# Squares of the differential heads summed in two rounded parts, and the next values' parts moved ahead, in a two-layer transformer kernel

## The chip, the cores and the metric

The kernel runs on one core of one Trainium2 chip. The metric is the device time of one execution in microseconds (us). The engines are TensorE (PE, matrix products; its weight loads are listed apart as PEld), VectorE (DVE), ScalarE (ACT), GpSimd (POOL) and SyncE (SP, which issues the DMAs). Each engine runs its own instruction list in order and waits on semaphores for the others.

## The reference, cut to what matters

Two transformer blocks are computed for 512 tokens of width 1024. The second block is where the change lies. It projects its normed input to two attentions, one with block selection (here a plain masked softmax of eight heads) and one with four differential heads:

```python
def diff_attention(q, k, v, lam, slopes):
    ...
        p = jax.nn.softmax(sc, axis=-1)
        a = p[:, :, 0] - lam * p[:, :, 1]
        return jnp.einsum('bhqk,bhkd->bhqd', a.astype(v.dtype), v)
...
d_out = rms_norm(d_out, diff_subln[layer]) * (1.0 - lambda_init)
...
mixed = jnp.concatenate([m_out, d_out], axis=-1)[:, :S]
x = x + jnp.einsum('bse,ed->bsd', mixed, w_out[layer])
```

The `rms_norm` of each differential head needs, for each token, the sum of the squares of the head's 128 outputs. That sum is what is changed.

## The kernel before, in words

All data lie transposed: 128 channels on the partitions, 512 tokens in a row. Large products are made in three terms: each operand is split into a rounded part of type fp32r (`_hi`) and the remainder (`_lo`), and TensorE adds high x high, low x high and high x low (lines 463 to 465, `products`). Plain f32 matmuls are used for transposes by the identity and for a few sums.

The second attention goes over eight chunks of 128 channels, c = 0 to 7. Even chunks are differential heads (`is_diff`), odd ones are pairs of ordinary heads. The loop `for c in range(0, KC, 2)` stands in the program of each engine, each with an order written out by hand, and all order between engines is by semaphores. What belongs to the pair c, c+1 around the change:

- `values2(c)` (PE) multiplies the transposed probabilities by the values into `OUT_BANK`; `raw_out(c)` (DVE, line 2267) copies that to `att2[:, 0]`; `square_out(c)` (ACT, line 1535) squares it into `d_sq`; `square_sum(c)` (PE) sums the squares over the partitions with a matrix of ones (line 1012, one f32 matmul of 512 columns) and adds an epsilon term that carries the softmax denominators, `rx_d`, by four f32 matmuls of 128 columns (line 1014); `variance(c)` (DVE) scales the sum to `d_v`; `first_root(c)` (ACT, lines 1540 and 1542) and `root(c)` (DVE, its first instruction writes `d_sq` from `d_y`) make the norm, and `gated_out(c)` (POOL, line 2547) applies the gate.
- The values of chunk c+2: `value_transposes(c + 2)` (PE, line 911) turns them, `stage_v2(c + 2)` (ACT, line 1495) makes `vd_hi`, `value_low(c + 2)` (DVE) makes `vd_lo` and raises `v2_lo_ready`. `value_half(c + 3, 0)` (PE, twelve matmuls of 512 columns) overwrites the bank that they read and so waits for `v2_lo_ready`.
- The probabilities of chunk c+1, first head: `transposes(c + 1, 0)` (PE, line 951, ten transposes) writes them to `PT_BANK`, `high_probs(c + 1, 0)` (ACT, line 1520) and `low_probs(c + 1, 0)` (DVE) split them. `transposes(c + 1, 1)` writes the second head's to the same bank, and waits for `low_probs(c + 1, 0)` by `ptl_ready`.

After the last pass PE forms the output projection by `out_chunks(t, first, last)`: t is the tile of the output and first, last are the mixed chunks it covers. `low_out(t)` (POOL, line 2563) makes the low part of its weights. `hold` on POOL is an instruction of one element (line 2518) that stands ahead of the remainders it makes (line 2521).

Of the kernel before, what the change touches and what calls it, by code (L numbers as in the profile page):

```python
# [8 lines left out]
F32R = mybir.dt.float32r  # L9
# [5 lines left out]
P = 128  # L15
# [65 lines left out]
def two_layer_block(nc, xT, vecs, wstream, outT):  # L81
    with ExitStack() as ctx:
# [12 lines left out]
        def sem(name):  # L95
            return ctx.enter_context(nc.semaphore(name))
# [120 lines left out]
        s2 = put("s2", [P, 2, 1280], F32)  # L217
        v_t = put("v_t", [P, T], F32)
        d_v = put("d_v", [P, T], F32)
        rx_d = put("rx_d", [P, TB, P], F32)  # L220
        rx_m = put("rx_m", [P, TB, P], F32)
        pt_hi = put("pt_hi", [P, 1280], F32R)
# [24 lines left out]
        def out_weights(t):  # L247
# [47 lines left out]
        out_read, raw_copied, dsq_ready, dss_ready, dvar_ready, drs_ready, d_final, att2_final, mixed_ready = (  # L295
            sem("out_read"), sem("raw_copied"), sem("dsq_ready"), sem("dss_ready"), sem("dvar_ready"),
            sem("drs_ready"), sem("d_final"), sem("att2_final"), sem("mixed_ready"))
        pool_held, gap_zeroed = sem("pool_held"), sem("gap_zeroed")
        first_done, first_sq, first_acc, first_drained = (
            sem("first_done"), sem("first_sq"), sem("first_acc"), sem("first_drained"))  # L300
# [159 lines left out]
        def _(pe):  # L460
# [420 lines left out]
            def value_half(c, half):  # L881

                if c >= KC:
                    return
                n = v_unit(c)
                if half == 0:
                    if c < 2:
                        pe.wait_ge(tile_drained, CREDIT + T_Q2 + 15 + c)
                    elif c == 2:
                        pe.wait_ge(g_drained, 1)  # L890
                    else:
                        pe.wait_ge(v2_lo_ready, c)
                    pe.wait_ge(lo_ready, n + 1)
                for k in range(4 * half, 4 * half + 4):
                    w = slice(k * P, (k + 1) * P)
                    mm = products(ps[:, v_bank(c), :], w_hi[:, n % 2, w], w_lo[:, n % 2, w], a_hi[:, k, :], a_lo[:, k, :],
                                  first=k == 0, last=k == KC - 1)
                if half:
                    mm.then_inc(units_done, 1)
# [106 lines left out]
            def square_sum(c):  # L1006

                if c >= KC:
                    return
                pe.wait_ge(dsq_ready, c // 2 + 1)  # L1010
                pe.wait_ge(rx_ready, c + 1)
                pe.matmul(ps[:, OUT_BANK, :], ones[:, :], d_sq[:, :], start=True, stop=False, skip_group_check=True)
                for b in range(TB):
                    mm = pe.matmul(ps[:, OUT_BANK, b * P:(b + 1) * P], rx_d[:, b, :], ident[:, :], start=False,
                                   stop=b == TB - 1, skip_group_check=True)
                mm.then_inc(dss_ready, 1)

            def out_chunks(t, first, last):

                high, low = out_weights(t)  # L1020
                if first == 0:
                    pe.wait_ge(lo_ready, U_W2 + t + 1)
                for n in range(first, last):
                    pe.wait_ge(mixed_ready, n + 1)
                    j = W2_ORDER[n]
                    w = slice(j * P, (j + 1) * P)
                    mm = products(ps[:, W2_BANKS[t], :], high[:, w], low[:, w], b_hi[:, j, :], b_lo[:, j, :],
                                  first=n == 0, last=n == KC - 1)
                if last == KC:
                    mm.then_inc(units_done, 1)  # L1030
# [34 lines left out]
            for c in range(0, KC, 2):  # L1065
                transposes(c)
                if c:
                    value_transposes(c + 1)
                scores2(c + 1, 0)
                if 0 < c < KC - 2:  # L1070
                    value_half(c + 2, 0)
                    value_half(c + 2, 1)
                    scores2(c + 1, 1)
                    gate_half(c + 1, 0)
                    scores2(c + 1, 2)
                    gate_half(c + 1, 1)
                else:
                    gate_half(c + 1, 0)
                    scores2(c + 1, 1)
                    gate_half(c + 1, 1)  # L1080
                    scores2(c + 1, 2)
                values2(c)
                value_transposes(c + 2)
                transposes(c + 1, 0)
                if c + 2 < KC:
                    square_sum(c)
                    value_half(c + 3, 0)
                    scores2(c + 2, 0)
                    transposes(c + 1, 1)
                    scores2(c + 2, 1)  # L1090
                    value_half(c + 3, 1)
                    scores2(c + 2, 2)
                    values2(c + 1, 0)
                    gate_part(c + 2, 0, 5)
                    values2(c + 1, 1)
                    den_rows(c + 1)
                    gate_part(c + 2, 5, KC)

            square_sum(KC - 2)
            pe.wait_ge(g_drained, KC)  # L1100
            out_chunks(0, 0, KC - 2)
            transposes(KC - 1, 1)
            values2(KC - 1, 0)
            pe.wait_ge(s2_biased, 4 * 16)
# [15 lines left out]
        def _(act):  # L1120
# [411 lines left out]
            def square_out(c):  # L1532

                act.wait_ge(raw_copied, c // 2 + 1)
                act.activation(d_sq[:, :], att2[:, 0, :], ACT.Square).then_inc(dsq_ready, 1)

            def first_root(c):
# [54 lines left out]
            for c in range(0, KC - 2, 2):  # L1592
                if c:
                    high_probs(c - 1, 1)
                    exponentials(c, 2)
                    high_mixed(c - 2)
                    split_unit(v_unit(c + 2))
                    split_unit(g_unit(c + 1))
                    stage_v2(c + 1)
                high_probs(c)  # L1600
                if c:
                    high_mixed(c - 1)
                exponentials(c + 1, 0)
                if c:
                    split_unit(v_unit(c + 3))
                exponentials(c + 1, 1)
                stage_qk2(c + 2)
                exponentials(c + 1, 2)
                square_out(c)
                stage_v2(c + 2)  # L1610
                high_probs(c + 1, 0)
                gate_sigmoid(c + 1)
                split_unit(g_unit(c + 2))
                gate_sigmoid(c)
                exponentials(c + 2, 0)
                first_root(c)
                exponentials(c + 2, 1)
                stage_qk2(c + 3)
# [29 lines left out]
        def _(dve):  # L1648
# [584 lines left out]
            def low_probs(c, head=0):  # L2233
                if c >= KC:
                    return
                dve.wait_ge(pth_ready, tq_of(c, head) + 1)
                low(pt_lo[:, :], psf[:, PT_BANK * 512:PT_BANK * 512 + 1280], pt_hi[:, :]).then_inc(ptl_ready, 1)
# [22 lines left out]
            def raw_out(c):  # L2260

                if c >= KC:
                    return
                dve.wait_ge(av2_ready, tq_of(c) + 1)
                if c:
                    dve.wait_ge(mixed_ready, c - 1)
                dve.tensor_copy(att2[:, 0, :], ps[:, OUT_BANK, :]).then_inc(raw_copied, 1)

            def variance(c):

                dve.wait_ge(dss_ready, c // 2 + 1)
                ts(d_v[:, :], ps[:, OUT_BANK, :], 1.0 / P, ALU.mult).then_inc(dvar_ready, 1)
# [44 lines left out]
            for c in range(0, KC, 2):  # L2317
                biased(c + 1, 0)
                low_probs(c)
                if c:  # L2320
                    value_drain(c + 2)
                den_small(c)
                den_spread(c)
                biased(c + 1, 1)
                if 0 < c < KC - 2:
                    biased(c + 1, 2)
                    gate2_drain(c + 1)
                else:
                    gate2_drain(c + 1)
                    biased(c + 1, 2)  # L2330
                raw_out(c)
                den_small(c + 1)
                den_spread(c + 1)
                slopes(c + 2)
                value_low(c + 2)
                variance(c)
                low_probs(c + 1, 0)
                biased(c + 2, 0)
                biased(c + 2, 1)
                value_drain(c + 3)  # L2340
                root(c)
                biased(c + 2, 2)
                low_probs(c + 1, 1)
                joined(c + 2, (3, 2, 0, 1))
                gate_row(c + 1)
                gate2_drain(c + 2)
                slopes(c + 3)
                value_low(c + 3)
                if c + 2 < KC:
                    gated(c + 1)  # L2350
# [355 lines left out]
```

## Time and profile before

| | |
|---|---|
| median of 3 runs | 1016.03 us (1015.81 to 1016.11) |
| profiled execution, its own time | 1016.16 us |
| its span | 1014.0 us |
| PE busy | 1002.1 us, 99% |
| DVE / ACT / POOL busy | 557.6 / 454.1 / 502.3 us |
| mean granted TensorE clock | 1.0 of full speed |

The span is the time from the first to the last instruction that the profiler recorded; the execution's own time is 2.2 us longer. Starts in the timeline are in us from the start of the span. Matmuls overlap in the pipeline: the time that one costs PE is the distance to the start of the next, not its own listed duration. In a bracket stands the time that the engine sat idle before an instruction and who ended it.

### The profile page before, as it was taken

How to read it: one execution, taken by the hardware profiler on the slowest of the kernel's cores; microseconds unless marked ns; L12 is line 12 of the kernel's file. 1: busy time of each engine (PE TensorE's matmuls, PEld its weight loads, DVE VectorE, ACT ScalarE, POOL GpSimd, SP SyncE). 2: the span in 40 equal slices, each digit the busy share in tenths (PEclk: the TensorE clock that was granted, in tenths of full speed). 3: DMA queues.
4: the chain of work that ended last, by engine and by line, in shares of the span. 5: the costliest groups of instructions: out<-in, count | busy, mean ns of one | idle time of the engine just before them, and what ended most of it. 6: DMA issues, size and time to landing. Idle time of an engine off the chain costs nothing.

```text
span 1014.0 us, 13704 instructions
## 1 busy us (share of the span) xinstructions
PE 1002.1 (99%) x5051; PEld 835.4 (82%) x5051; DVE 557.6 (55%) x943; ACT 454.1 (45%) x682; POOL 502.3 (50%) x296
## 2 busy tenths in 40 slices
PE   9999999999999999999999999999999999999998
PEld 7888888888888988888888888889888778777787
DVE  6799897887633964334334310116715276676731
ACT  7222346898644532322322322233454347667630
POOL 4444365842346134444444465453387545755562
PEclk9999999999999999999999999999999999999999
DMA  7232222212244032332322323333132120111112
GB/s 258 83 104 93 95 83 67 80 63 84 73 176 151 17 102 86 103 101 85 103 100 87 103 104 104 104 123 106 43 104 83 63 84 22 64 63 43 42 63 83
DMA packets 26402, 91.11 MB, mean 90 GB/s; under 512 B 3056, under 2 KB 3184, under 8 KB 26224
## 3 DMA queue, kind: packets, MB, share of 16 engines
q1 hardware_dynamic: 26352, 90.42, 26.4%
q8 instruction: 34, 0.56, 0.2%
q14 instruction: 16, 0.13, 0.0%
HBM read 88.31 MB, written 2.10 MB: 89 GB/s over the span
## 4 chain that ended last, share of the span: by engine, by line
PE 89%; DVE 7%; ACT 2%; issue 1%; DMA 1%; POOL 0%; SPq 0%; DVEq 0%
PE ps L463 27%; PE ps L465 27%; PE ps L464 27%; PE ps L927 2%; PE ps L951 1%; DVE resid L2014 1%; PE ps L624 1%; PE ps L640 1%; DVE a_lo L1664 1%; DMA resid<-x_t 1%; DVE sq_x L1657 1%; DVE q_raw L1657 1%; DVE mix L1657 1%; DVE b_lo L1664 1%; PE ps L656 0%
## 5 line engine op out<-in xcount | busy, mean ns | idle before, releaser
L2362 POOL TENSOR_TENSOR w_lo<-w_raw,w_hi 128x1024 fp32r<-128x1024 f32 x137 | 325.8, 2379 | 410.6 <-ACT w_hi L1128 357.9
L1128 ACT ACTIVATE w_hi<-w_raw 128x1024 fp32r<-128x1024 f32 x133 | 139.2, 1047 | 279.6 <-PE ps L465 279.6
L463 PE MATMUL ps<-a_hi,w_hi 128*128 128x512 f32 (+1 forms) x544 | 211.6, 389 | 4.6 <-DVE v_lo L1661 3.1
L465 PE MATMUL ps<-a_hi,w_lo 128*128 128x512 f32 (+1 forms) x544 | 207.0, 380 | 0.0
L464 PE MATMUL ps<-a_lo,w_hi 128*128 128x512 f32 (+1 forms) x544 | 206.8, 380 | 0.0
L463 PE MATMUL ps<-b_hi,w_hi 128*128 128x512 f32 x392 | 152.9, 390 | 0.0
L465 PE MATMUL ps<-b_hi,w_lo 128*128 128x512 f32 x392 | 152.6, 389 | 0.0
L464 PE MATMUL ps<-b_lo,w_hi 128*128 128x512 f32 x392 | 152.5, 389 | 0.0
L463 PEld LDWEIGHTS ps<-a_hi,w_hi 128*128 128x128 f32 x544 | 102.3, 188 | 28.3 <-DVE v_lo L1661 4.4
L465 PEld LDWEIGHTS ps<-a_hi,w_lo 128*128 128x128 f32 x544 | 102.3, 188 | 20.0
L464 PEld LDWEIGHTS ps<-a_lo,w_hi 128*128 128x128 f32 x544 | 102.4, 188 | 18.3 <-issue 0.2
L463 PEld LDWEIGHTS ps<-b_hi,w_hi 128*128 128x128 f32 x392 | 73.6, 188 | 15.2
L464 PEld LDWEIGHTS ps<-b_lo,w_hi 128*128 128x128 f32 x392 | 73.6, 188 | 15.2
L465 PEld LDWEIGHTS ps<-b_hi,w_lo 128*128 128x128 f32 x392 | 73.6, 188 | 15.2
L1741 DVE SCALAR_TENSOR_TENSOR ps<-u_pad,vec,ps 128x512 f32<-128x512 f32 x112 | 75.4, 747 | 0.0
L463 PE MATMUL ps<-h_hi,w_hi 128*128 128x512 f32 (+1 forms) x186 | 69.2, 372 | 0.0
L464 PE MATMUL ps<-h_lo,w_hi 128*128 128x512 f32 (+1 forms) x186 | 69.0, 371 | 0.0
L465 PE MATMUL ps<-h_hi,w_lo 128*128 128x512 f32 (+1 forms) x186 | 69.0, 371 | 0.0
L1657 DVE TENSOR_TENSOR up_h<-up_u,up_s 128x512 f32<-128x512 f32 x22 | 51.3, 2330 | 21.2 <-ACT up_s L1387 21.1
L1657 DVE TENSOR_TENSOR up_u<-ps,scale_row 128x512 f32<-128x512 f32 x22 | 15.2, 690 | 82.0 <-PE ps L465 82.0
L1657 DVE TENSOR_TENSOR sq_f<-sq_f 128x512 f32<-128x512 f32 x13 | 12.5, 960 | 82.7 <-ACT sq_f L1411 82.0
L1508 ACT ACTIVATE s<-s,smax 128x384 f32<-128x384 f32 (+2 forms) x64 | 35.2, 552 | 16.9 <-DVE smax L2187 16.9
(339 smaller groups left out, 1727.1 us busy)
## 6 DMA issues: line engine op xcount, KB each, us to landing
w_raw<-weights SPq DMA_DIRECT2D x156, 512.0 KB, 3.2
resid<-x_t SPq DMA_DIRECT2D x8, 256.0 KB, 6.6
w_raw<-weights SPq DMA_DIRECT2D x8, 256.0 KB, 6.6
resid<-x_t SPq DMA_DIRECT2D x1, 2048.0 KB, 8.8
out_t<-out_sb SPq DMA_DIRECT2D x8, 256.0 KB, 2.0
vec<-vecs SPq DMA_DIRECT2D x1, 220.0 KB, 7.1
vec<-vecs SPq DMA_DIRECT2D x1, 4.0 KB, 1.6
```

The lines of the kernel that those rows point to most:

```text
L463: pe.matmul(out, s_hi, m_hi, start=first, stop=False, skip_group_check=True)
L464: pe.matmul(out, s_hi, m_lo, start=False, stop=False, skip_group_check=True)
L465: return pe.matmul(out, s_lo, m_hi, start=False, stop=last, skip_group_check=True)
L624: pe.matmul(z_of(h)[:, o:o + (b + 1) * P], q[r, tok], k[r, keys], start=b != 0 and t == 0, stop=False, skip_group_check=True)
L640: mm = pe.transpose(z_of(h)[:, o:o + P], neg_log[:, src:src + P], ident[:, :])
L927: mm = pe.matmul(scores_of(part, head, b), q2[rows, tok], k2[rows, keys], start=n == 0 and t == 0, stop=False, skip_group_check=True)
L1128: act.activation(w_hi[:, k % 2, 0:width], w_raw[:, k, 0:width], ACT.Copy).then_inc(hi_ready, 1)
L1508: e = act.activation(s2[:, head, w], s2[:, head, w], ACT.Exp, scale=-1.0, bias=smax[:, head, b:b + 1], accum_out=den[:, kind_of(c), half_o ...
L1657: return dve.tensor_tensor(out, in0, in1, op)
L1664: return dve.scalar_tensor_tensor(out=out, in0=in0, scalar=scale, in1=high.bitcast(F32), op0=ALU.mult, op1=ALU.subtract)
L1741: V.do(dve.scalar_tensor_tensor(out=acc if k == TAPS - 1 else part, in0=src, scalar=w, in1=part, op0=ALU.mult, op1=ALU.add))
L2362: pool.tensor_tensor(w_lo[:, k % 2, 0:width], w_raw[:, k, 0:width], w_hi[:, k % 2, 0:width].bitcast(F32), ALU.subtract).then_inc(lo_ready, 1)
```

## The change

The square sum is made from two parts. ACT writes the square twice, rounded to fp32r (`d_hi`) and in f32 (`d_sq`); DVE subtracts them to `d_lo` (`square_low`); PE sums both parts with two fp32r matmuls of 512 columns in place of one f32 matmul. The two new tiles lie in the places of `d_v` and `d_y`, which are not in use then.

The orders change. PE: `value_half(c + 3, 0)` stands ahead of `square_sum(c)` in the passes c = 0, 2, 4; after the last pass, `out_chunks(0, 0, KC - 2)` stands ahead of `square_sum(KC - 2)`. ACT: `stage_v2(c + 2)` stands ahead of `square_out(c)`. DVE: `value_low(c + 2)` stands right behind `raw_out(c)`, ahead of the denominators, then `square_low(c)`; in the last pass alone, `variance` stands behind `low_probs`.

```diff
+        d_hi = place("d_hi", [P, T], F32R, at["d_v"])
+        d_lo = place("d_lo", [P, T], F32R, at["d_y"])
...
-                pe.wait_ge(dsq_ready, c // 2 + 1)
+                pe.wait_ge(dsq_lo, c // 2 + 1)
                 pe.wait_ge(rx_ready, c + 1)
-                pe.matmul(ps[:, OUT_BANK, :], ones[:, :], d_sq[:, :], start=True, stop=False, skip_group_check=True)
+                pe.matmul(ps[:, OUT_BANK, :], ones[:, :].bitcast(F32R), d_hi[:, :], start=True, stop=False, skip_group_check=True)
+                pe.matmul(ps[:, OUT_BANK, :], ones[:, :].bitcast(F32R), d_lo[:, :], start=False, stop=False, skip_group_check=True)
...
                 if c + 2 < KC:
+                    value_half(c + 3, 0)
                     square_sum(c)
-                    value_half(c + 3, 0)
                     scores2(c + 2, 0)
                     transposes(c + 1, 1)
...
-            square_sum(KC - 2)
             pe.wait_ge(g_drained, KC)
             out_chunks(0, 0, KC - 2)
+            square_sum(KC - 2)
             transposes(KC - 1, 1)
...
                 act.wait_ge(raw_copied, c // 2 + 1)
+                act.activation(d_hi[:, :], att2[:, 0, :], ACT.Square).then_inc(dsq_hi, 1)
                 act.activation(d_sq[:, :], att2[:, 0, :], ACT.Square).then_inc(dsq_ready, 1)
...
                 exponentials(c + 1, 2)
+                stage_v2(c + 2)
                 square_out(c)
-                stage_v2(c + 2)
                 high_probs(c + 1, 0)
...
+            def square_low(c):
+                dve.wait_ge(dsq_hi, c // 2 + 1)
+                dve.wait_ge(dsq_ready, c // 2 + 1)
+                low(d_lo[:, :], d_sq[:, :], d_hi[:, :]).then_inc(dsq_lo, 1)
...
                 raw_out(c)
+                value_low(c + 2)
                 den_small(c + 1)
                 den_spread(c + 1)
+                square_low(c)
                 slopes(c + 2)
-                value_low(c + 2)
-                variance(c)
+                if c + 2 < KC:
+                    variance(c)
                 low_probs(c + 1, 0)
+                if c + 2 == KC:
+                    variance(c)
                 biased(c + 2, 0)
```

## Rows read from the trace of the kernel before

**Rows 1.** The page, part 1: busy us (share of span) x instructions

```profile
PE 1002.1 (99%) x5051; PEld 835.4 (82%) x5051; DVE 557.6 (55%) x943; ACT 454.1 (45%) x682; POOL 502.3 (50%) x296
```

**Rows 2.** Whom PE waited for, 700 to 1014: us in total, times, longest

```profile
PE ps L463 <- DVE v_lo L1661: 3.1, 3, 1.0
```

**Rows 3.** Timeline of PE, pass c = 0: start us, us, instruction, count

```profile
839.70 0.62 PE L911 MATMUL ps<-ident,v_t 128*128 128x128 f32 x4
...
841.31 1.12 PE L1012 MATMUL ps<-d_sq,ones 128*128 128x512 f32 x2
842.27 1.05 PE L1014 MATMUL ps<-ident,rx_d 128*128 128x128 f32 x8
843.08 0.48 PE L463 MATMUL ps<-a_hi,w_hi 128*128 128x512 f32 x1
...
846.91 1.31 PE L951 MATMUL ps<-ident,s 128*128 128x128 f32 x10
```

**Rows 4.** Timeline of ACT, pass c = 0

```profile
840.62 0.63 ACT L1535 ACTIVATE d_sq<-att 128x512 f32<-128x512 f32 x1 [0.55 <-DVE att L2267]
841.16 0.58 ACT L1495 ACTIVATE vd_hi<-ps 128x512 fp32r<-128x512 f32 x1
841.63 1.23 ACT L1520 ACTIVATE pt_hi<-ps 128x1280 fp32r<-128x1280 f32 x1
```

**Rows 5.** Timeline of DVE, pass c = 0

```profile
841.77 0.69 DVE L1661 TENSOR_TENSOR vd_lo<-ps,vd_hi 128x512 fp32r<-128x512 f32 x1 [0.15 <-ACT vd_hi L1495]
843.36 0.69 DVE L1653 TENSOR_SCALAR d_v<-ps 128x512 f32<-128x512 f32 x1 [0.90 <-PE ps L1014]
843.97 1.48 DVE L1661 TENSOR_TENSOR pt_lo<-ps,pt_hi 128x1280 fp32r<-128x1280 f32 x1
```

**Rows 6.** Timeline of PE: a wait for a value's low part, passes 0 to 2

```profile
866.14 0.50 PE L463 MATMUL ps<-a_hi,w_hi 128*128 128x512 f32 x1 [1.03 <-DVE v_lo L1661]
866.48 0.39 PE L464 MATMUL ps<-a_lo,w_hi 128*128 128x512 f32 x1
866.71 0.40 PE L465 MATMUL ps<-a_hi,w_lo 128*128 128x512 f32 x1
```

**Rows 7.** Timeline of DVE, 863 to 883

```profile
863.30 2.18 DVE L1653 TENSOR_SCALAR bias<-dist,small 128x512 f32<-128x512 f32 x1
865.40 0.68 DVE L1661 TENSOR_TENSOR v_lo<-ps,v_hi 128x512 fp32r<-128x512 f32 x1
...
882.06 1.24 DVE L2231 COPY rx_m<-den 128x512 f32<-128x512 f32 x1
```

**Rows 8.** Timeline of PE, pass c = 2

```profile
882.63 1.12 PE L1012 MATMUL ps<-d_sq,ones 128*128 128x512 f32 x2
...
888.25 1.31 PE L951 MATMUL ps<-ident,s 128*128 128x128 f32 x10
```

**Rows 9.** Timeline of POOL, 862 to 884

```profile
862.82 4.91 POOL L2362 TENSOR_TENSOR w_lo<-w_raw,w_hi 128x1024 fp32r<-128x1024 f32 x2
...
881.74 1.28 POOL L2521 TENSOR_TENSOR b_lo<-att,b_hi 128x512 fp32r<-128x512 f32 x1
```

**Rows 10.** Timeline of PE, last pass and behind it

```profile
959.82 1.12 PE L1012 MATMUL ps<-d_sq,ones 128*128 128x512 f32 x2 [0.33 <-ACT d_sq L1535]
...
975.24 0.45 PE L463 MATMUL ps<-b_hi,wo_hi 128*128 128x512 f32 x1
```

**Rows 11.** Timeline of ACT, behind the last pass

```profile
963.59 0.61 ACT L1540 ACTIVATE d_y<-d_v 128x512 f32<-128x512 f32 x1
```

**Rows 12.** Timeline of DVE, behind the last pass

```profile
961.88 0.69 DVE L1653 TENSOR_SCALAR d_v<-ps 128x512 f32<-128x512 f32 x1 [2.20 <-PE ps L1014]
...
964.90 2.12 DVE L1657 TENSOR_TENSOR d_sq<-d_y 128x512 f32<-128x512 f32 x1 [0.94 <-ACT d_y L1542]
```

**Rows 13.** Timeline of POOL, behind the last pass

```profile
969.16 1.30 POOL L2547 TENSOR_TENSOR att<-att,gate_e 128x512 f32<-128x512 f32 x1 [2.68 <-DVE att L2284]
...
971.67 4.76 POOL L2563 TENSOR_TENSOR wo_lo<-w_raw,wo_hi 128x1024 fp32r<-128x1024 f32 x2
```

More of the change, by code:

```diff
@@ L297, in two_layer_block @@
             sem("drs_ready"), sem("d_final"), sem("att2_final"), sem("mixed_ready"))
+        dsq_hi, dsq_lo = sem("dsq_hi"), sem("dsq_lo")
         pool_held, gap_zeroed = sem("pool_held"), sem("gap_zeroed")
```

## The prediction

> **What bounds the kernel now.** I read four views, in this order. The page's busy times first: PE is busy for 1002.1 of 1014.0 us, and no other engine reaches 56% [rows 1]. So the time is PE's own list: what is taken from it comes off, and each new wait of PE is added. Next PE's waits: in the stretch of the second attention they are few, three of 1.0 us each for a value's low part [rows 2] and one of 0.33 us for the squares in the last pass [rows 10]. Nearly nothing can be gained there. Third the timelines of PE around the change [rows 3, 8]: the reader is to see the distances from start to start. Last the timelines of ACT, DVE and POOL at the same place [rows 4, 5, 9]: they say when each semaphore that PE asks for is raised, and so how long PE could come earlier, or be sent elsewhere, before it waits.
>
> **Part 1, the square sum itself.** The f32 matmul with the ones starts at 841.31 and the next line at 842.27: it costs PE 0.96 us [rows 3]. An fp32r matmul of 512 columns costs 0.23 (866.48 to 866.71), and the first of a run 0.34 (866.14 to 866.48) [rows 6]; a run of twelve is 0.34 + 11 x 0.23 = 2.87 us. The pair stands behind such products and costs 0.46. Saved: 0.50 us in each of four passes, 2.0 us if nothing else moved. Loading the ones twice is inside that distance, as every product's weight load is. The matmuls with `rx_d` stay f32 and cost 0.81 us (842.27 to 843.08) [rows 3]. They now stand between two fp32r stretches, so there is one longer first distance more, 0.1 us, where it matters below.
>
> **Part 2, `value_half` ahead of `square_sum` (passes 0, 2, 4).** `value_half(c + 3, 0)` waits for `vd_lo`. Before, it came at 843.08, when `vd_lo` had been ready since 841.77 + 0.69 = 842.46 [rows 3, 5]. Now PE asks at 841.31. When is it ready in the new orders? The value transposes end at 839.70 + 0.62 = 840.32 [rows 3]; ACT is free from 840.62 - 0.55 = 840.07 and takes `vd_hi` first, 840.36 to 840.94 with its 0.58 us [rows 4]; `raw_out` on DVE is over before (ACT took its copy at 840.62) [rows 4], so `value_low` runs 840.97 to 841.66 with its 0.69 [rows 5]; from the end of such a low part to PE's start are 0.06 us (865.40 + 0.68 = 866.08, then 866.14) [rows 6, 7]. PE starts `value_half` at 841.72: a new wait of 0.41 us, which alone takes back most of the 0.50.
>
> **Part 3, `variance` still ahead of `low_probs`: the term that decides.** In the passes 0, 2 and 4 DVE runs `variance(c)`, which waits for PE's square sum, and only then `low_probs(c + 1, 0)`; PE's `transposes(c + 1, 1)` waits for the latter. Before, the low part of the probabilities was made at 843.97 + 1.48 = 845.45, and PE came for it at 846.91, 1.46 us later [rows 3, 5]: that slack hid the chain. Now the square sum stands 2.87 us further back. Worked out for pass 0:
>
> - `value_half` from 841.72, 2.87 us: the pair starts at 844.59, `rx_d` at 845.05.
> - From the first `rx_d` matmul to the start of `variance` are 843.36 - 842.27 = 1.09 us: 846.14. From there to `low_probs` 0.61 (843.36 to 843.97): 846.75. It lasts 1.48: 848.23 [rows 3, 5].
> - PE starts `transposes(c + 1, 1)` 0.06 later, at 848.29, in place of 846.91 [rows 3]: **1.38 us later**.
> - PE itself would come at 846.91 - 0.50 + 0.41 = 846.82, or 846.9 with the new boundary. So its new wait there is about 1.4 us, for the low part of the probabilities.
>
> Pass 2 has the same distance from the square sum to the transposes (888.25 - 882.63 = 5.62, against 5.60) [rows 3, 8] and gives the same, and the third of these passes, c = 4, repeats the second. Three times 1.38 is **+4.1 us**. PE has no idle time behind to take it up: the three waits of 1.0 us [rows 2] come from DVE and POOL work that PE's own products release (POOL's weight remainder began at 862.82, DVE's bias at 863.30 took 2.18) [rows 7, 9], and move along.
>
> The added work on ACT and DVE is hidden, and this is its cover. ACT's second square costs its distance, 0.54 (840.62 to 841.16), and is done by about 842.0 [rows 4]; `high_probs` then ends near 843.2, 3.5 us ahead of `low_probs`. DVE's `square_low` reads two f32 tiles of 512; the nearest row is `vd_lo`'s 0.69 [rows 5]. It is done by about 842.8, or 843.4 if it yields to POOL once (below), with PE asking at 844.59. Without that cover each would cost its 0.5 to 0.7 us on the chain, three times.
>
> **Part 4, the last pass.** PE no longer waits 0.33 us for the squares, since `out_chunks(0, ...)` goes first, and saves the 0.50: it comes about 0.8 us earlier to what follows [rows 10]. `low_probs` is ahead of `variance` here, so nothing waits as in part 3. But `variance(6)` is now released behind 18 more products (0.34 + 17 x 0.23 = 4.25 us). PE is free at 959.82 - 0.33 = 959.49 [rows 10], the products end at 963.74, the pair takes 0.46 and `variance` starts 1.09 later, at 965.3 against 961.88 [rows 12]. Before, POOL's `gated_out` followed it by 969.16 - 961.88 = 7.28 us [rows 12, 13], of which 1.02 was `first_root` behind other work of ACT (963.59 against 962.57) [rows 11, 12] and 1.44 the first instruction of `root` (2.12 against the 0.68 that such a tile takes in [rows 7]). Those two fall away: 965.3 + 4.8 = 970.1, 0.95 later than before. POOL's next steps follow it, so the low weights of output tile 2, done at 971.67 + 4.76 / 2 = 974.05 [rows 13], are done at 975.0. PE asked at 975.24 [rows 10] and now would at 974.4. It waits until 975.0, and of 0.8 us 0.2 are left: **-0.2 us**. Bounds: nothing is left, or all 0.8 if POOL is not held up by the later norm.
>
> **Sum.** +4.1 - 0.2 = +3.9 us on the profiled execution (1014.0 span, 1016.16 in all). It lies 0.13 us from the median of the runs, so the prediction is 1016.03 + 3.9 = **1019.9 us**, 0.38% slower.
>
> **A resource the sum leaves out: who yields, DVE or POOL.** The trace shows DVE work that reads and writes the memory by itself being held up by POOL. The bias at 863.30 took 2.18 us, beside POOL's remainder that ran from 862.82 [rows 7, 9], and `rx_m` took 1.24 us from 882.06, ending 0.3 behind POOL's remainder (881.74 + 1.28 = 883.02) [rows 7, 9]. In the passes 2 and 4 the moved `rx_m` and the new `square_low` fall on POOL's `q_lo` and `k_lo`, remainders of the same size as that one. If DVE gets its turn first or after one of them, `d_lo` is there by 885.5, and PE asks at 885.9 (844.59, and 882.63 - 841.31 = 41.32 from pass to pass [rows 3, 8]). If it lets both pass, at 1.3 us each from 883.1, and then takes 0.69, `d_lo` comes near 886.5 and the chain of part 3 is 0.7 longer in two passes.
>
> The Trainium skill, "SBUF — State Buffer", section "Who interferes with whom", has this as a rule: a DVE instruction with two inputs in the memory contends with a POOL instruction that reads it, and the loser blocks for the whole instruction. This trace agrees: the square of `d_y`, with both inputs there, took 2.12 us. By that rule the new `square_low` is such an instruction and `vd_lo`, whose first input is in PSUM, is not; without it the sum is the 1019.9 above, and with it anything from there to the first rival.
>
> **The rivals.**
>
> - *POOL passes DVE twice.* As just worked out, 2 x 0.7 = 1.4 us more: 1021.3 us. For it: `rx_m` already lost once. Against it: after the one remainder in its way `rx_m` was done within 0.3 us, so DVE was next in turn and POOL was not let through twice.
> - *The variance is hidden anyway, not slower than before.* It decides if `low_probs(c + 1, 0)` ends before PE arrives, at 846.9 or earlier, 1.3 us before I have it; DVE would have to get the square sum that much sooner. Then passes 0, 2, 4 give 0.50 - 0.41 = 0.1 each in gain and the last 0.2 to 0.8: 1015.2 us, within 0.2% (2.0 us, about what a measurement of this kernel tells from no change). Against it: each link is an in-order list and a semaphore, and the durations stand in the trace.
> - *The clean gain.* If also `vd_lo` came before PE asks (0.41 us sooner), all four passes keep their 0.50 and the 0.33 goes: 1016.03 - 2.3 = 1013.7 us.
> - *The pair costs no less than the f32 matmul*, so the change does not do what it says: 4 x 0.5 more, 1021.9 us. The distance of 0.23 between fp32r matmuls of this very size [rows 6] speaks against it.
>
> **How the numbers follow.** Forecast 0.82; POOL passes twice 0.08; hidden anyway 0.06; clean gain 0.02; pair not cheaper 0.02. Faster by over 0.2% 0.02, within 0.2% 0.07 (the hidden case, and a hundredth of the forecast), slower 0.91. The range goes from 1018.4 (the wait of part 3 half a microsecond shorter in each pass) to 1021.4 (the first rival, and a little). Outside it are the other three cases and the edges of the forecast, 0.15 in all.
>
> **What would show it.** In the profile after: new waits of PE at line 951's transposes of the second head for `pt_lo`, three of about 1.4 us, in the first two passes at about 848.3 and 891.0; waits of PE for `vd_lo` of about 0.4 us, three; the pair of fp32r matmuls at 0.23 us each; no wait before the sum in the last pass, and one near 0.6 us before output tile 2. The distance from the start of the first `rx_d` matmul to that of `variance` stays 1.09. The prediction is wrong if `pt_lo` still ends before PE gets there, or if PE's idle time grows by more than these and is charged to `d_lo`.

## The result, and the profile after

The changed kernel takes 1020.1 us (median of 6 runs, 1019.83 to 1021.77) against 1016.0 us of the kernel before on the same chips. The ratio is 1.0044, with a 95% interval of 1.0034 to 1.0054: slower by 0.44%. Predicted were 1019.9 us, with 1018.4 to 1021.4 as range. The profiled execution has a span of 1018.4 us, 4.4 more than before.

PE's waits in the kernel after come first: whom PE waited for over the whole span, us in total, times, longest. "..." stands for lines left out.

```profile
PE ps L954 <- DVE pt_lo L1666: 4.1, 3, 1.4
PE ps L466 <- DVE v_lo L1666: 3.1, 3, 1.0
...
PE ps L466 <- DVE vd_lo L1666: 1.0, 3, 0.3
PE ps L495 <- DVE sq_x L1662: 0.7, 1, 0.7
...
PE ps L466 <- POOL wo_lo L2578: 0.3, 1, 0.3
```

The wait for `v_lo` is the one of [rows 2], unchanged. Those for `pt_lo`, `vd_lo` and `wo_lo` are new, and they are the three new waits of the prediction. The wait for `d_sq` [rows 10] is gone. The one for `sq_x` stands near the start of the kernel (below). The timeline of PE in pass 0 of the kernel after, which answers to [rows 3]:

```profile
840.12 0.62 PE L914 MATMUL ps<-ident,v_t 128*128 128x128 f32 x4
840.58 1.25 PE L954 MATMUL ps<-ident,s 128*128 128x128 f32 x10
842.16 0.49 PE L466 MATMUL ps<-a_hi,w_hi 128*128 128x512 f32 x1 [0.32 <-DVE vd_lo L1666]
...
844.99 0.40 PE L1015 MATMUL ps<-d_hi,ones 128*128 128x512 f32 x1
845.23 0.40 PE L1016 MATMUL ps<-d_lo,ones 128*128 128x512 f32 x1
845.47 1.05 PE L1018 MATMUL ps<-ident,rx_d 128*128 128x128 f32 x8
846.45 0.50 PE L930 MATMUL ps<-k_hi,q_hi 64*128 64x512 f32 x2
...
848.79 1.28 PE L954 MATMUL ps<-ident,s 128*128 128x128 f32 x10 [1.38 <-DVE pt_lo L1666]
```

And the timeline of DVE in the same pass, which answers to [rows 5], with the row of ACT that makes the high part of the probabilities behind it:

```profile
841.41 0.69 DVE L1666 TENSOR_TENSOR vd_lo<-ps,vd_hi 128x512 fp32r<-128x512 f32 x1 [0.40 <-ACT vd_hi L1499]
...
842.95 0.68 DVE L1666 TENSOR_TENSOR d_lo<-d_sq,d_hi 128x512 fp32r<-128x512 f32 x1
843.55 0.47 DVE L1658 TENSOR_SCALAR bias_h<-dist,small 128x512 f32<-128x512 f32 x1
846.56 0.69 DVE L1658 TENSOR_SCALAR d_v<-ps 128x512 f32<-128x512 f32 x1 [2.54 <-PE ps L1018]
847.17 1.48 DVE L1666 TENSOR_TENSOR pt_lo<-ps,pt_hi 128x1280 fp32r<-128x1280 f32 x1
```

```profile
842.31 1.24 ACT L1524 ACTIVATE pt_hi<-ps 128x1280 fp32r<-128x1280 f32 x1
```

Read together they show the chain from one engine to the other: DVE has nothing to do for 2.54 us, although the probabilities wait to be split (their high part was there at 842.31 + 1.24 = 843.55), because `d_v` stands first in its list and waits for PE's square sum. Then `d_v` and `pt_lo` follow, and PE waits 1.38 us for `pt_lo`.

Where the 4.4 us are: from the start of the value transposes to that of the second head's transposes PE needs 8.67 us in pass 0 (840.12 to 848.79) against 7.21 before (839.70 to 846.91 [rows 3]), so 1.46 more. The passes 2 and 4 give 8.71 each. Of the kernel after:

```profile
882.87 0.63 PE L914 MATMUL ps<-ident,v_t 128*128 128x128 f32 x4
...
887.77 0.40 PE L1015 MATMUL ps<-d_hi,ones 128*128 128x512 f32 x1
...
891.58 1.28 PE L954 MATMUL ps<-ident,s 128*128 128x128 f32 x10 [1.38 <-DVE pt_lo L1666]
...
925.68 0.63 PE L914 MATMUL ps<-ident,v_t 128*128 128x128 f32 x4
...
934.39 1.28 PE L954 MATMUL ps<-ident,s 128*128 128x128 f32 x10 [1.38 <-DVE pt_lo L1666]
...
963.00 1.28 PE L954 MATMUL ps<-ident,s 128*128 128x128 f32 x10
...
979.63 0.50 PE L466 MATMUL ps<-b_hi,wo_hi 128*128 128x512 f32 x1 [0.32 <-POOL wo_lo L2578]
```

Of the kernel before:

```profile
881.02 0.63 PE L911 MATMUL ps<-ident,v_t 128*128 128x128 f32 x4
...
922.36 0.63 PE L911 MATMUL ps<-ident,v_t 128*128 128x128 f32 x4
...
929.57 1.31 PE L951 MATMUL ps<-ident,s 128*128 128x128 f32 x10
...
958.21 1.28 PE L951 MATMUL ps<-ident,s 128*128 128x128 f32 x10
```

Before, the distance was 7.23 in pass 2 (881.02 to 888.25 [rows 8]) and 7.21 in pass 4 (922.36 to 929.57), so these two give 1.48 and 1.50: 4.4 us in all. In the last pass the distance from `transposes(7, 0)` to output tile 2 fell from 17.03 (958.21 to 975.24) to 16.63 (963.00 to 979.63), -0.4. The sum is +4.0. The other 0.4 us of the span lie ahead of the change: the first pass starts its value transposes 0.42 later (840.12 against 839.70), after a wait for `sq_x` near the start of the kernel of 0.74 us in this execution against 0.20 in that of before. That wait differs between executions with the same work there: it is 0.3 us in the profile of orders_only and 0.8 in that of low_probs_first (both below). The medians are 4.1 us apart, near the 4.0 that the change itself gives.

### The profile page after: what moved, and what is told of

It reads as the page before. It is cut to its first block, busy times and chain, and to the rows that moved or that the text cites. A ratio compares the mean times of both kernels' runs of the same rounds, so it can differ in the third digit from the quotient of the medians.

```text
span 1018.4 us, 13716 instructions
## 1 busy us (share of the span) xinstructions
PE 1001.4 (98%) x5051; PEld 836.2 (82%) x5051; DVE 561.5 (55%) x947; ACT 456.3 (45%) x686; POOL 502.3 (49%) x296
## 4 chain that ended last, share of the span: by engine, by line
PE 87%; DVE 8%; ACT 2%; POOL 1%; issue 1%; DMA 1%; SPq 0%; DVEq 0%; POOLq 0%
PE ps L466 27%; PE ps L468 26%; PE ps L467 26%; PE ps L930 2%; DVE resid L2019 1%; PE ps L954 1%; PE ps L627 1%; DMA resid<-x_t 1%; PE ps L643 1%; DVE a_lo L1669 1%; DVE sq_x L1662 1%; DVE q_raw L1662 1%; DVE mix L1662 1%; DVE b_lo L1669 1%; PE ps L659 0%
```

## The experiments

The eight variants were timed in five rounds beside the kernel before; the first row repeats the comparison above. "Ratio" is to that kernel, with its 95% interval. The kernel before had a median of 1016.0 us beside the changed kernel, 1015.78 in the next four comparisons (low_probs_first to third_square) and 1015.59 in the last four, so differences of a few tenths between rows are best read from the ratios and the traces.

| kernel | median us | ratio |
|---|---|---|
| changed kernel | 1020.1 | 1.0044 [1.0034, 1.0054] |
| low_probs_first | 1015.51 | 0.9997 [0.9988, 1.0006] |
| orders_only | 1021.48 | 1.0055 [1.0041, 1.0068] |
| split_only | 1021.0 | 1.0052 [1.0038, 1.0066] |
| third_square | 1020.22 | 1.0044 [1.0030, 1.0058] |
| orders_low_first_no_split | 1016.87 | 1.0014 [1.0005, 1.0023] |
| variance_twice | 1023.57 | 1.0089 [1.0075, 1.0103] |
| slopes_early | 1013.93 | 0.9983 [0.9974, 0.9992] |
| all_three | 1015.04 | 0.9995 [0.9986, 1.0004] |

**low_probs_first: one line of DVE's order.**

```diff
-                if c + 2 < KC:
-                    variance(c)
                 low_probs(c + 1, 0)
-                if c + 2 == KC:
-                    variance(c)
+                variance(c)
```

> The changed kernel with variance behind low_probs in all four passes on DVE; nothing else differs. If the cost is the order of variance ahead of low_probs (my theory), the three waits of TensorE for pt_lo of 1.38 us each in the changed kernel go, the waits for vd_lo of 0.3 us stay, and the time is 1020.1 - 4.1 = 1016.0 us, the time of before within 0.5. If instead the added square on ScalarE and the added subtraction on VectorE are what costs, the waits stay and the time is 1020 within 0.5.

Measured: 1015.51 us, 4.6 below the changed kernel. All of the loss is gone with this one order, within the interval. Of PE's waits, those for `pt_lo` are gone and the others stay:

```profile
PE ps L466 <- DVE v_lo L1666: 3.1, 3, 1.0
PE ps L466 <- DVE vd_lo L1666: 1.0, 3, 0.3
```

DVE's timeline in pass 0 shows the order: the low part at 843.37, 2.6 us ahead of the variance. PE is at its transposes at 846.77 without a wait, 7.23 us behind the start of the value transposes (839.54), against 8.67 in the changed kernel and 7.21 before. Rows of DVE, then of PE:

```profile
843.37 1.48 DVE L1666 TENSOR_TENSOR pt_lo<-ps,pt_hi 128x1280 fp32r<-128x1280 f32 x1
845.99 0.69 DVE L1658 TENSOR_SCALAR d_v<-ps 128x512 f32<-128x512 f32 x1 [1.14 <-PE ps L1018]
```

```profile
846.77 1.31 PE L954 MATMUL ps<-ident,s 128*128 128x128 f32 x10
```

The rival, that the added instructions cost, falls: they are all still there.

**orders_only: the new orders without the split.** The sum is one f32 matmul again, PE waits for `d_sq` itself, and `d_hi` and `square_low` are left out.

```diff
-                pe.wait_ge(dsq_lo, c // 2 + 1)
+                pe.wait_ge(dsq_ready, c // 2 + 1)
...
-                pe.matmul(ps[:, OUT_BANK, :], ones[:, :].bitcast(F32R), d_hi[:, :], start=True, stop=False, ...)
-                pe.matmul(ps[:, OUT_BANK, :], ones[:, :].bitcast(F32R), d_lo[:, :], start=False, stop=False, ...)
+                pe.matmul(ps[:, OUT_BANK, :], ones[:, :], d_sq[:, :], start=True, stop=False, ...)
...
-                act.activation(d_hi[:, :], att2[:, 0, :], ACT.Square).then_inc(dsq_hi, 1)
...
-                square_low(c)
```

> The changed kernel with all its new orders, but the squares summed by the one f32 matmul as before (no d_hi, no d_lo). My theory: the matmul costs 0.96 us against 0.48 for the pair and lies on the chain to variance and low_probs in three passes and on TensorE's own list in the last, so 4 x 0.48 = 1.9 us more than the changed kernel: 1022.0 us. Rival, the split itself costs (more work on ScalarE and VectorE): 1018 us or less.

Measured: 1021.48 us, 1.4 above the changed kernel by the medians. The direction is that of the theory, the size a little less than 1.9. The intervals of the two ratios overlap, so the direction rests on the trace: in pass 0 PE needs 9.06 us from the value transposes to those of the second head (839.52 to 848.58) where the changed kernel needs 8.67. The rival's 1018 us or less is far outside. PE's timeline in pass 0 says why it is less than 1.9: behind fp32r products the f32 matmul costs 0.86 us (844.39 to 845.25), not the 0.96 that it cost behind the f32 transposes [rows 3].

```profile
844.39 1.02 PE L1015 MATMUL ps<-d_sq,ones 128*128 128x512 f32 x2
845.25 1.05 PE L1017 MATMUL ps<-ident,rx_d 128*128 128x128 f32 x8
```

So the split is worth 0.38 us in a pass in this order, 1.5 in four.

**split_only: the split without the new orders.** The same three additions (`d_hi`, `square_low` ahead of `slopes`, the pair of matmuls) in the kernel before.

```diff
                 den_spread(c + 1)
+                square_low(c)
                 slopes(c + 2)
```

> The kernel before with its own orders and the split alone: d_hi and d_sq on ScalarE, square_low on VectorE ahead of slopes, two fp32r matmuls. My theory: the square sum is asked for right behind the transposes, at 841.3 in pass 0, and d_lo is not there before 842.5, since a second square (0.54) and a subtraction (0.69) stand in front: a wait of 1.2 us or more in each of four passes against 0.48 saved, so 0.8 to 1.4 us more each, 1019.3 to 1021 us (1019.6 the likeliest). Rival, the split is a gain wherever it stands: 1016.0 - 1.9 = 1014.1 us.

Measured: 1021.0 us, at the upper end of the theory, 1.4 above its likeliest value, and far from the rival. PE waits for `d_lo` in every pass, 5.8 us together, and for `vd_lo` in two:

```profile
PE ps L1015 <- DVE d_lo L1666: 5.8, 4, 1.7
PE ps L466 <- DVE vd_lo L1666: 0.8, 2, 0.4
```

The waits for `d_lo` are 1.69, 1.21, 1.21 and 1.65 us. In the passes 2 and 4 it is the 1.2 of the theory, and the 0.4 for `vd_lo`, which the theory did not have, comes on top. In pass 0 `d_lo` took 1.17 us instead of 0.68 beside POOL's `k_lo`, which ends at 840.59 + 1.26 = 841.85. In the last pass 0.33 us of the wait were there before [rows 10]. Rows of DVE and of POOL in pass 0:

```profile
841.23 1.17 DVE L1666 TENSOR_TENSOR d_lo<-d_sq,d_hi 128x512 fp32r<-128x512 f32 x1 [0.65 <-ACT d_sq L1540]
```

```profile
840.59 1.26 POOL L2533 TENSOR_TENSOR k_lo<-y_qk,k_hi 128x512 fp32r<-128x512 f32 x1
```

The move of `value_half` gives the split the time in which the two parts are made.

**third_square: more of ACT's added work.**

```diff
+                A.do(act.activation(d_hi[:, :], att2[:, 0, :], ACT.Square))
+                A.wait()
                 act.activation(d_hi[:, :], att2[:, 0, :], ACT.Square).then_inc(dsq_hi, 1)
```

> The changed kernel with the square into d_hi written twice on ScalarE (0.6 us of added work in each pass, same result). My theory: ScalarE's added work is hidden, pt_hi comes 3 us ahead of its low part; no change, 1020.1 us within 0.4, and the waits for pt_lo stay 1.38 us. Rival, ScalarE's added work is on the chain: 4 x 0.6 = 2.4 us more, 1022.5 us.

Measured: 1020.22 us, no change. The waits for `pt_lo` are the same 4.1 us; only in the last pass PE's wait for the weights of tile 2 went from 0.3 to 0.7 us.

**orders_low_first_no_split: good orders, no split.** Both edits above, `low_probs_first` and `orders_only`, together.

> The orders of the changed kernel, variance behind low_probs in all passes, and the squares summed by one f32 matmul as before (no split). My theory: against the kernel before, three passes pay the wait for vd_lo (0.32 us) and a second boundary between f32 and fp32r (0.1), the last pass gives and takes about nothing: 1.3 us more, 1017.1 us; so the split itself is worth 4 x 0.4 to 0.5 = 1.6 to 2 us against low_probs_first. Rival, the split is worth nothing once the orders are good: 1015.5 us like low_probs_first.

Measured: 1016.87 us, 1.4 above low_probs_first (by the ratios 1.0014 against 0.9997, 1.7). The split is worth about 1.5 us in this setting too, and the moved order without it is a small loss against the kernel before. The traces of pass 0 agree: from the value transposes to those of the second head PE needs 7.60 us here (838.58 to 846.18), against 7.21 in the kernel before and 7.23 in low_probs_first. The moved order costs 0.39 us in such a pass, and the split gives 0.37 back.

**variance_twice: the suspected chain made longer.**

```diff
                 dve.wait_ge(dss_ready, c // 2 + 1)
+                if c + 2 < KC:
+                    V.do(ts(d_v[:, :], ps[:, OUT_BANK, :], 1.0 / P, ALU.mult))
+                    V.wait()
                 ts(d_v[:, :], ps[:, OUT_BANK, :], 1.0 / P, ALU.mult).then_inc(dvar_ready, 1)
```

> The changed kernel with the variance made twice, one after the other, on VectorE in the passes 0, 2 and 4 (same result). My theory: what stands between the square sum and low_probs adds to the time one for one; the added instruction costs about 0.7 us, the waits for pt_lo grow from 1.38 to about 2.1, and the time is 1020.1 + 3 x 0.7 = 1022.2 us. Rival, the wait for pt_lo has another cause and VectorE has room there: 1020.1 us.

Measured: 1023.57 us, 1.4 above the expectation. The waits grew as expected, from 4.1 to 6.3 us:

```profile
PE ps L954 <- DVE pt_lo L1666: 6.3, 3, 2.1
```

The rest goes with a lower clock of TensorE. In pass 4 the transposes start after a wait of 2.10 us, and take 1.86 us to the next start where the changed kernel's pass 0 needs 1.22 (848.79 to 850.01):

```profile
935.90 1.94 PE L954 MATMUL ps<-ident,s 128*128 128x128 f32 x10 [2.10 <-DVE pt_lo L1666]
937.76 0.69 PE L930 MATMUL ps<-k_hi,q_hi 64*128 64x384 f32 x2
```

The windows of PE around it (us, busy and count, granted clock, DMA share, GB/s):

```profile
932.00:934.00 2.00, 1.79 (x15) 1.00 0.00 0
934.00:936.00 2.00, 0.10 (x1) 1.00 0.01 4
936.00:938.00 2.00, 2.00 (x12) 0.59 0.55 195
938.00:940.00 2.00, 2.00 (x14) 0.56 0.17 68
940.00:945.00 5.00, 5.00 (x30) 1.00 0.00 0
```

Between 936.5 and 939.5 the granted clock was 0.50, which is the lower of its two levels, 1.2 GHz against 2.4. From the start of these transposes to the next value product PE needs 3.65 us (935.90 to 939.55), in pass 0 of the same execution, at full clock, 2.21 (848.83 to 851.04): 1.44 us more, which is the 1.4 above the expectation. All five runs of this kernel have a mean clock below 0.999, from 0.995 to 0.998, and the two longest of them have the lowest; none of the 27 runs of the kernel before beside it is below 0.999.

**slopes_early: on top of low_probs_first, the wait that was there before.** The 3.1 us for `v_lo` [rows 2] are in every kernel. DVE's `slopes(c + 3)`, 2.18 us beside POOL's remainder [rows 7], stands ahead of the low part that PE waits for.

```diff
+                slopes(c + 3)
                 gate_row(c + 1)
                 gate2_drain(c + 2)
-                slopes(c + 3)
                 value_low(c + 3)
```

> low_probs_first with slopes(c + 3) ahead of gate_row(c + 1) on VectorE, where GpSimd has only started on the next remainders. The three waits of 1.0 us for v_lo stand in both kernels; before the low part VectorE's slopes take 2.17 us beside GpSimd's weight remainder, against 0.47 alone. My theory (the wait is VectorE held up by GpSimd): the low part comes 0.5 us sooner, bounded then by v_hi, and the time is 1015.5 - 1.5 = 1014.0 us. Rival, the wait is set by ScalarE's v_hi: no change.

Measured: 1013.93 us, as expected, and faster than the kernel before by 0.17% with an interval clear of one. The wait is halved, and what ends DVE's idle time ahead of the low part is now ACT's `v_hi`:

```profile
PE ps L466 <- DVE v_lo L1666: 1.6, 3, 0.5
```

```profile
864.61 0.69 DVE L1666 TENSOR_TENSOR v_lo<-ps,v_hi 128x512 fp32r<-128x512 f32 x1 [1.47 <-ACT v_hi L1501]
```

**all_three: two more moves.** The value transposes go into the middle of `values2`, and the high and low weights of output tile 2 are made ahead of `first_root(6)` on ACT and of `gated_out(6)` on POOL.

```diff
-                values2(c)
-                value_transposes(c + 2)
+                values2(c, middle=lambda: value_transposes(c + 2))
...
             split_unit(U_W2 + 1)
+            split_out(2)
             first_root(KC - 2)
...
             low_out(1)
+            low_out(2)
             gated_out(KC - 2)
             gate_silu(KC - 1)
-            low_out(2)
             low_out(3)
```

> slopes_early and two more moves: the value transposes in the middle of values2 (vd_hi, and so vd_lo, sooner), and the weights of output tile 2 split on ScalarE ahead of first_root(6) and on GpSimd ahead of gated_out(6). Theory: the waits for vd_lo (3 x 0.32) go at the price of 3 x 0.1 for a boundary, and the wait of 0.32 for the weights of tile 2 goes: 0.9 us less than slopes_early, 1013.1 us, a gain over the kernel before of 0.27%. Rival: the value transposes wait for the gate's drain in the middle of the products, and the gain is nothing.

Measured: 1015.04 us, 1.1 worse than slopes_early, and the runs of the two do not overlap (1014.5 us and more against 1014.42 and less). Both moves missed, and neither for the rival's reason. ACT could not start `vd_hi` sooner: `values2` still reads the `vd_hi` of two chunks before, so `stage_v2` waits for its last product, and that now comes later. `vd_hi` starts 2.67 us behind the first product of `values2` (837.22), where it started 2.62 behind in slopes_early (837.47 to 840.09).

```profile
839.89 0.60 ACT L1500 ACTIVATE vd_hi<-ps 128x512 fp32r<-128x512 f32 x1 [0.33 <-PE ps L468]
```

In the last pass POOL's weight remainder now falls on `root(6)` of DVE, whose first instruction takes 2.84 us in place of 0.69 in slopes_early; the low part of the probabilities stands behind it, and PE waits 1.2 us for that in place of 0.3 for the weights. Rows of DVE, of POOL and of PE's waits:

```profile
965.24 2.84 DVE L1663 TENSOR_TENSOR d_sq<-d_y 128x512 f32<-128x512 f32 x1 [1.36 <-ACT d_y L1548]
```

```profile
965.12 2.41 POOL L2576 TENSOR_TENSOR wo_lo<-w_raw,wo_hi 128x1024 fp32r<-128x1024 f32 x1
```

```profile
PE ps L988 <- DVE pt_lo L1667: 1.2, 1, 1.2
```

The best version is slopes_early.

## Why the prediction was right

**Part 1, the pair.** Right: 0.24 us each (844.99, 845.23, 845.47) where I had 0.23, and the distance from `rx_d` to `variance` stayed 1.09 us (845.47 to 846.56). The saving is 0.48 us against the order before, where I had 0.50, and 0.38 once the sum stands behind fp32r products (orders_only).

**Part 2, the wait for `vd_lo`.** The start came where it was put, 2.04 us behind that of the value transposes (840.12 to 842.16, predicted 839.70 to 841.72, 2.02). The wait itself reads 0.32 and not 0.41, since the profile counts it from the modelled end of the transposes before.

**Part 3, `variance` ahead of `low_probs`.** Right, and it accounts for the whole loss: with that order turned round the loss is gone (low_probs_first), and with the chain 0.7 us longer the waits grow by 0.7 each (variance_twice). The term was 1.38 us a pass and measured 1.46 to 1.50. The difference in pass 0 is the last step: from the end of `pt_lo` (847.17 + 1.48 = 848.65) to PE's start at 848.79 are 0.14 us, where I took 0.06 from a start of fp32r products. The cover of the added work held too: third_square changed nothing, and PE never waited for `d_lo`.

**Part 4, the last pass.** Forecast -0.2, measured -0.4. The wait for tile 2 was 0.3 and not 0.6. I had PE free at 959.49, the modelled end of the transposes; the products really follow 1.03 us behind their start (963.00 to 964.03), where 959.49 is 1.28 behind it. The whole chain to POOL's weights starts 0.25 us sooner for that.

**The sum.** +3.9 against +4.1 by the medians. The two small misses work against each other (+0.3 in part 3, -0.2 in part 4).

**Who yields, DVE or POOL.** In pass 2 DVE was held up twice and it cost nothing. The timeline of DVE, then of POOL:

```profile
885.00 1.55 DVE L2236 COPY rx_m<-den 128x512 f32<-128x512 f32 x1
886.48 0.68 DVE L1666 TENSOR_TENSOR d_lo<-d_sq,d_hi 128x512 fp32r<-128x512 f32 x1
887.08 1.52 DVE L1658 TENSOR_SCALAR bias_h<-dist,small 128x512 f32<-128x512 f32 x1
```

```profile
884.98 1.29 POOL L2536 TENSOR_TENSOR q_lo<-y_qk,q_hi 128x512 fp32r<-128x512 f32 x1
...
886.56 1.75 POOL L2536 TENSOR_TENSOR k_lo<-y_qk,k_hi 128x512 fp32r<-128x512 f32 x1
```

`rx_m` let one remainder of POOL pass (884.98 + 1.29 = 886.27) and then had its turn, `d_lo` followed at once and was there at 887.16, and PE asked at 887.77. So the first rival did not come about, with 0.6 us to spare. `d_lo` itself was not held up here; in split_only, where it fell on POOL's `k_lo`, it was. The rival's price was a little low: behind two remainders of POOL `rx_m` would have needed its own time too (0.49 us in pass 0 of the kernel before) ahead of `d_lo`, so the chain would have been about 1.0 longer (an estimate from these rows) and not 0.7. The other rivals are refuted by the waits and by the pair's 0.48 us. What the hidden variance would have given can be seen, since low_probs_first makes it so: 1015.51 us, where that rival had 1015.2. With the larger wait away the change is level with the kernel before: what the pair saves, the waits for `vd_lo`, the added change between f32 and fp32r and the wait for the weights take back. In pass 0 that is 0.37 us given and 0.39 taken (orders_low_first_no_split), of which the wait for `vd_lo` reads 0.32; the last pass was not taken apart.

## What to carry to other kernels

When an instruction on the busiest engine is put behind other work, follow its result through the in-order list of the engine that takes it: what stands behind the taker there is late too, though it has nothing to do with it. Here a cheaper matmul and a free place for it were right, and one scaling instruction of 0.69 us, left ahead of a 1.48 us one that PE needed sooner, cost over 4 us. A list of who would wait, made for each moved step before it is moved, finds this, and so does a profile where an engine idles 2.5 us with ready work behind the instruction that waits.

## What the runs showed of the hardware

After a wait of PE of 2.10 us in variance_twice's third pass (c = 4) the granted clock was 0.50 for some 3 us, and PE's work cost 1.44 us more. After waits of the same 2.10 us in its first two passes the clock stayed at 1.00, and the ten transposes cost 1.21 and 1.22 us instead of 1.86. One of the six runs of the changed kernel, with waits of 1.38 us in the profiled one, has a mean clock of 0.998 and took 1021.77 us, 1.7 above the median; no trace shows whether that was the same thing. A wait of PE can thus be followed by a loss beyond its own length, and not every time; what decides it stays open.

An f32 matmul of 512 columns costs PE 0.96 us behind f32 transposes and 0.86 behind fp32r products; an fp32r one costs 0.23 to 0.24, and 0.34 as the first of a run [rows 6]. In pass 2 of the changed kernel DVE and POOL held each other up: DVE's `rx_m` took 1.55 us beside POOL's `q_lo`, where it took 0.49 in pass 0 of the kernel before, and POOL's next remainder took 1.75 us, with DVE's `d_lo` under way at its start, instead of 1.29.
